# Giving each tile of the split weight ring its own offset in SBUF

## Chip, cores and metric

One core of a Trainium2 chip runs the whole kernel. The metric is the device time of one execution in microseconds.

## What is computed

One decoder layer in float32 over 256 tokens of width 2048. Three token mixers share one input projection, and their results are gated, added and projected; a SwiGLU feed-forward of width 5632 follows. Cut to what matters:

```python
h = rms_norm(x, attn_norm_g)
da_q, da_k, da_v, r_q, r_k, r_v, r_g, m_q, gates = split(h @ w_in)        # w_in: 2048 x 13312
o_da  = diff_attention(da_q, da_k, da_v, ...)      # causal, 8 heads, two softmax maps each
o_ret = retention(r_q, r_k, r_v, r_g, ...)         # 8 heads, chunks of 128
o_mem = memory_attention(m_q, mem @ w_mem_kv, ...) # 4 heads of 256
merged = sum(sigmoid(gate_b) * (o_b @ w_o_b) for b in (da, ret, mem))
x = x + merged @ w_out
hf = rms_norm(x, ffn_norm_g)
out = x + (silu(hf @ w_ffn_gate) * (hf @ w_ffn_up)) @ w_ffn_down
```

## The kernel before

Nearly all work is products of 256 tokens with float32 weight matrices. Each product is done at the rate of the rounded format fp32r and nearly to float32 accuracy: a value is split into a rounded part ("hi") and the remainder ("lo"), and hi x hi, hi x lo and lo x hi are added in PSUM (`three_passes`, the matmul of L1010).

The tokens' columns are the stationary operand. They lie transposed in `hT_hi`, `hT_lo` (normed input of a projection) and `oT_hi`, `oT_lo` (outputs of the mixers, then activations), each `[128, 16, 256]`; a block of 128 tokens by 128 columns of k is 512 bytes in each partition. The weights are the moving operand and go through a ring of four slots (`RING`). A slot holds a pair: two tiles of 128 rows (k) by 512 columns, 2,048 bytes a tile in each partition. There are three rings: `raw` as loaded, `w_hi` rounded, `w_lo` the remainder.

For each pair g, in slot s % 4:

- SyncE's queue waits until VectorE has made the remainder of pair g-4 (`lo_done`) and loads 512 KB into `raw` (L212);
- ScalarE waits for the load and until TensorE has used pair g-4 (`pair_used`), and copies `raw` to `w_hi`, which rounds it (`high`, L337; L374 for the first four);
- VectorE waits for that and writes `raw` - `w_hi` into `w_lo` (`low`, L625; L658 for the first four);
- TensorE waits for that (`lo_done`) and issues 12 matmuls: two tiles of the pair (k), two blocks of tokens (t), three passes (n). In each tile the order is hi x hi, hi x lo, lo x hi, so `w_hi`, `w_lo`, `w_hi`.

There are 584 pairs: 32 for the memory's keys and values, 16 + 96 for the projections of the mixers, 3 x 48 for gates and output projections, 32 for `w_out`, and 264 for the feed-forward (16 at its start, ten steps of 24, 8 at its end). Between pairs, at fixed places of the pair loops, stand the small matmuls and the transposes of the attention parts (L1032, L1070, L1085 and others) and, on ScalarE and VectorE, evacuations and softmax work. TensorE's output goes to two accumulators of two PSUM banks each.

The tensors `raw`, `w_hi`, `w_lo`, `hT_hi`, `hT_lo`, `oT_hi`, `oT_lo` are allocated first, in this order, at 16 KB a partition each, then `proj` (the projections, 56 KB), `kvm` and the small ones. Every tile of the rings is then a multiple of 2,048 bytes from the ring's start, and the tensors are multiples of 16,384 bytes apart.

Of the kernel before, what the change touches and what calls it, by code (L numbers as in the profile page):

```python
# [26 lines left out]
F32 = mybir.dt.float32  # L27
F32R = mybir.dt.float32r
I32 = mybir.dt.int32
ALU = mybir.AluOpType  # L30
ACT = mybir.ActivationFunctionType
AX = mybir.AxisListType

P = 128
# [3 lines left out]
NCOL = 512  # L38
# [18 lines left out]
RING = 4  # L57
# [8 lines left out]
ROUND = 12582912.0  # L66


def shape_constants():

    da = np.float32(DA_THETA) ** (-np.arange(DA_ROT // 2, dtype=np.float32) * np.float32(2.0) / np.float32(DA_ROT))
    rt = np.float32(RT_THETA) ** (-np.arange(RT_D // 2, dtype=np.float32) * np.float32(2.0) / np.float32(RT_D))
    lg = np.log(np.float32(1.0) - np.float32(2.0) ** (np.float32(-5.0) - np.arange(RT_H, dtype=np.float32)))
    return np.concatenate([da, rt, lg]).astype(np.float32)[None, :]


def program(nc, x, mem, positions, w_in, da_q_norm_g, da_k_norm_g, da_lambda_q1, da_lambda_k1,
# [6 lines left out]
    with ExitStack() as ctx:  # L84
        def sb(name, shape, dt=F32):
            return ctx.enter_context(nc.sbuf_tensor(name, shape, dt))
# [3 lines left out]


        raw = sb("raw", [P, RING, 2, NCOL])
        w_hi = sb("w_hi", [P, RING, 2, NCOL], F32R)
        w_lo = sb("w_lo", [P, RING, 2, NCOL], F32R)
        hT_hi = sb("hT_hi", [P, KD, TOK], F32R)
        hT_lo = sb("hT_lo", [P, KD, TOK], F32R)
        oT_hi = sb("oT_hi", [P, KD, TOK], F32R)
        oT_lo = sb("oT_lo", [P, KD, TOK], F32R)
        proj = sb("proj", [P, TB, GATE0])
        kvm = sb("kvm", [P, TB, D])  # L100
        sq = sb("sq", [P, TB, 2, 256])
# [55 lines left out]
        acc = [ctx.enter_context(nc.psum_tensor(f"acc{i}", [P, TB, NCOL], F32)) for i in range(2)]  # L157
        at = ctx.enter_context(nc.psum_tensor("at", [P, 4, 512], F32))
# [3 lines left out]
        hi_done, lo_done = sem("hi_done"), sem("lo_done")  # L162
# [167 lines left out]
        def _(act):  # L330
            def high(g, s):


                act.wait_ge(loaded[s % RING],
                            (g // RING + 2) * 16 if isinstance(g, int) else g * 4 + (32 - 4 * (s % RING)))
                act.wait_ge(pair_used, g + 1)
                act.activation(w_hi[:, s % RING], raw[:, s % RING], ACT.Copy).then_inc(hi_done, 1)  # L337

            def row_squares(k, t, ready, c0):

# [30 lines left out]

            for s in range(RING):
                act.wait_ge(loaded[s], 16)
                act.activation(w_hi[:, s], raw[:, s], ACT.Copy).then_inc(hi_done, 1)  # L374
                if s == 0:
                    act.wait_ge(gains_in, 16)
                    act.wait_ge(memT_in[0], 16)
                    high_input(0, range(2), oT_hi, memT)
                for n in range(1, 4):
                    if MEM_PIECES[n][0] == 2 + 2 * s:  # L380
                        act.wait_ge(memT_in[n], 16)
                high_input(0, range(2 + 2 * s, 4 + 2 * s), oT_hi, memT)


            for s in range(32):
# [8 lines left out]
                if s in (13, 15, 23, 31):  # L394
                    if s == 13:
                        act.wait_ge(row_root, 2)
                    n = (s - 6) // 8 if s == 13 else s // 8
# [27 lines left out]
            with act.Fori(0, MEM_H) as i:  # L425
                for s in range(16):
# [11 lines left out]
                    if s == 6:  # L438
                        act.wait_ge(M["negmax"], i + 1)
                        for t in range(TB):  # L440
                            e = act.activation(pm[:, t, 0:256], at[:, 2, t * 256:(t + 1) * 256], ACT.Exp,
                                               bias=nmx[:, 0, t:t + 1], scale=MEM_D ** -0.5,
                                               accum_out=den[:, 0, t:t + 1])
# [72 lines left out]
            with act.Fori(0, 4) as i:  # L516
                for s in range(12):
                    if s == 0:
                        for j in range(2):
                            e = act.activation(dec[:, j, 0:256], rel[:], ACT.Exp,  # L520
                                               scale=sc[:, ds(i * 2 + (NROT + j), 1)])
# [94 lines left out]
        def _(v):  # L616
# [5 lines left out]
            def low(g, s):  # L622

                v.wait_ge(hi_done, g + (RING + 1))
                v.tensor_tensor(w_lo[:, s % RING], raw[:, s % RING], w_hi[:, s % RING].bitcast(F32),  # L625
                                ALU.subtract).then_inc(lo_done, 1)

            def row_means(k):
# [26 lines left out]

            for s in range(RING):
                v.wait_ge(hi_done, s + 1)
                v.tensor_tensor(w_lo[:, s], raw[:, s], w_hi[:, s].bitcast(F32), ALU.subtract).then_inc(lo_done, 1)  # L658
                low_input(0, range(2 + 2 * s if s else 0, 4 + 2 * s), oT_lo, oT_hi, memT)

            for s in range(32):
# [49 lines left out]
            with v.Fori(0, MEM_H) as i:  # L711
                for s in range(16):
                    if s == 0:
# [3 lines left out]
                        for t in range(TB):  # L717
                            for k, src in enumerate((proj[:, t, ds(i * MEM_D + MQ0, MEM_D)],
                                                     kvm[:, t, ds(i * MEM_D, MEM_D)])):
                                e = v.scalar_tensor_tensor(out=qn[:, t, k, :], in0=src,  # L720
                                                           scalar=rstd[:, 2 * t + k:2 * t + k + 1],
                                                           in1=g_mem[:, k, :], op0=ALU.mult, op1=ALU.mult)
# [212 lines left out]
            for s in range(32):  # L935
# [4 lines left out]
                if s % 8 == 7:  # L940
                    n = s // 8
# [64 lines left out]
        def _(pe):  # L1006
            def three_passes(s, hi, lo, k0, p, k, t, first, last):
                tok = slice(t * P, (t + 1) * P)
                for n, (a, w) in enumerate(((hi, w_hi), (hi, w_lo), (lo, w_hi))):
                    e = pe.matmul(acc[p][:, t, :], a[:, k0 + k, tok], w[:, s % RING, k, :],  # L1010
                                  start=first and k == 0 and n == 0, stop=last and k == 1 and n == 2)
                return e

# [265 lines left out]
```

## Time and profile before

| | |
|---|---|
| median of 3 runs | 1676.9 us (1676.47 to 1677.61) |
| span of the profiled execution, first to last instruction | 1674.9 us |
| TensorE matmuls busy | 1668.0 us, 7,592 |
| VectorE busy | 950.0 us (57%) |
| ScalarE busy | 774.7 us (46%) |
| bytes read from HBM | 317.31 MB, 191 GB/s over the span |

The profiled execution's own device time isn't given apart from its span; the median of the runs lies 2.0 us above the span, which is what lies around it. Busy matmuls are pipelined and overlap, so a busy TensorE says only that it has work at all times, and the distance between the starts of two matmuls is what one costs.

### The profile page before, as it was taken

To read this page: it belongs to the slowest core of one execution; us is meant where nothing else is said; L and a number is where in the kernel's file an instruction comes from. 1 tells how busy PE (TensorE), PEld (TensorE's weight loads), DVE (VectorE), ACT (ScalarE), POOL (GpSimd) and SP (SyncE) were. 2 spreads that over 40 slices of the span, in tenths; PEclk is the share of its full clock that TensorE was granted. 3 is DMA by queue.
4 is the path that set the end of the run, shared out by engine and by line. 5 is a ranking of instruction groups with operands and counts; after the bars stand their busy time and mean duration, and the time that the engine had idled before them with its cause. 6 is when DMAs were issued, how large, how long until landed. Compare 5 with 4: busy or idle time off the path is not lost.

```text
span 1674.9 us, 21891 instructions
## 1 busy us (share of the span) xinstructions
PE 1668.0 (100%) x7592; PEld 1381.3 (82%) x7592; DVE 950.0 (57%) x1061; ACT 774.7 (46%) x936; POOL 31.9 (2%) x33
## 2 busy tenths in 40 slices
PE   9999999999999999999999999999999999999999
PEld 7888888888888888888888888888888888888887
DVE  5565554454577766655555545565554554655555
ACT  6655454444555544444444544444434444444342
POOL 0000000000111000000000000000000000000000
PEclk9999999999999999999999999999999999999999
DMA  9876555566544565666655666666666666666664
GB/s 340 265 217 187 176 169 168 177 196 192 174 152 150 180 185 175 213 199 190 188 184 184 186 189 192 191 193 188 188 192 190 190 192 188 189 192 191 192 189 151
DMA packets 167095, 319.96 MB, mean 191 GB/s; under 512 B 11152, under 2 KB 15760, under 8 KB 166288
## 3 DMA queue, kind: packets, MB, share of 16 engines
q1 hardware_dynamic: 167056, 319.45, 62.1%
q8 instruction: 24, 0.39, 0.1%
q14 instruction: 15, 0.12, 0.0%
HBM read 317.31 MB, written 2.10 MB: 191 GB/s over the span
## 4 chain that ended last, share of the span: by engine, by line
PE 91%; issue 7%; DVE 1%; DMA 0%; POOL 0%; ACT 0%; DVEq 0%; ACTq 0%; SPq 0%; POOLq 0%
PE acc L1010 87%; PE at L1032 2%; POOL rstd L315 0%; PE at L1070 0%; PE at L1085 0%; DMA raw<-in_w_mem_kv 0%; DVE w_lo L625 0%; DMA raw<-in_w_in 0%; ACT pm L486 0%; PE at L1160 0%; DVE ss L650 0%; ACT w_hi L337 0%; PE at L1172 0%; PE at L1173 0%; PE at L1171 0%
## 5 line engine op out<-in xcount | busy, mean ns | idle before, releaser
L625 DVE TENSOR_TENSOR w_lo<-raw,w_hi 128x1024 fp32r<-128x1024 f32 x580 | 706.7, 1224 | 639.5 <-ACT w_hi L337 637.6
L337 ACT ACTIVATE w_hi<-raw 128x1024 fp32r<-128x1024 f32 x580 | 614.6, 1061 | 829.4 <-PE acc L1010 812.7
L1010 PE MATMUL acc<-w_hi,hT_hi 128*128 128x512 f32 x1568 | 616.7, 393 | 0.0
L1010 PE MATMUL acc<-w_hi,hT_lo 128*128 128x512 f32 x1568 | 611.0, 390 | 0.0
L1010 PE MATMUL acc<-w_lo,hT_hi 128*128 128x512 f32 x1568 | 610.5, 389 | 0.0
L1010 PEld LDWEIGHTS acc<-w_hi,hT_hi 128*128 128x128 f32 x1568 | 294.5, 188 | 62.2 <-issue 1.3
L1010 PEld LDWEIGHTS acc<-w_hi,hT_lo 128*128 128x128 f32 x1568 | 294.4, 188 | 61.9
L1010 PEld LDWEIGHTS acc<-w_lo,hT_hi 128*128 128x128 f32 x1568 | 294.6, 188 | 59.8
L1010 PE MATMUL acc<-w_hi,oT_hi 128*128 128x512 f32 x768 | 300.9, 392 | 1.2 <-DVE oT_lo L644 1.2
L1010 PE MATMUL acc<-w_hi,oT_lo 128*128 128x512 f32 x768 | 299.1, 389 | 0.0
L1010 PE MATMUL acc<-w_lo,oT_hi 128*128 128x512 f32 x768 | 299.0, 389 | 0.0
L1010 PEld LDWEIGHTS acc<-w_hi,oT_hi 128*128 128x128 f32 x768 | 144.2, 188 | 31.4 <-issue 1.6
L1010 PEld LDWEIGHTS acc<-w_hi,oT_lo 128*128 128x128 f32 x768 | 144.2, 188 | 30.1
L1010 PEld LDWEIGHTS acc<-w_lo,oT_hi 128*128 128x128 f32 x768 | 144.3, 188 | 29.4
L927 DVE TENSOR_TENSOR proj<-acc,proj 128x1024 f32<-128x1024 f32 x47 | 57.6, 1225 | 20.6 <-PE acc L1010 20.6
L315 POOL TENSOR_TENSOR rstd<-ms,minus_half 128x4 f32<-128x4 f32 (+1 forms) x16 | 26.9, 1680 | 613.4 <-DVE ms L651 613.4
L365 ACT ACTIVATE proj<-acc,row_rstd 128x512 f32 (+1 forms) x28 | 17.7, 685 | 23.6 <-PE acc L1010 23.6
L951 DVE SCALAR_TENSOR_TENSOR proj<-acc,row_rstd,proj 128x512 f32<-128x512 f32 x22 | 15.5, 747 | 5.9 <-PE acc L1010 5.9
L1032 PEld LDWEIGHTS at<-ident,proj 128*128 128x128 f32 x120 | 14.0, 140 | 2.0
L1032 PE MATMUL at<-ident,proj 128*128 128x128 f32 x120 | 15.5, 272 | 0.0
L650 DVE TENSOR_REDUCE ss<-sq 128x4 f32<-128x512 f32 (+2 forms) x16 | 15.1, 946 | 0.0
L472 ACT ACTIVATE proj<-acc,half_rstd 128x512 f32<-128x512 f32 x24 | 15.1, 681 | 0.0
(151 smaller groups left out, 474.9 us busy)
## 6 DMA issues: line engine op xcount, KB each, us to landing
raw<-in_w_in SPq DMA_DIRECT2D x208, 512.0 KB, 3.9
raw<-in_w_ffn_gate SPq DMA_DIRECT2D x88, 512.0 KB, 3.8
raw<-in_w_ffn_up SPq DMA_DIRECT2D x88, 512.0 KB, 3.7
raw<-in_w_ffn_down SPq DMA_DIRECT2D x88, 512.0 KB, 3.8
raw<-in_w_mem_kv SPq DMA_DIRECT2D x32, 512.0 KB, 6.5
raw<-in_w_out SPq DMA_DIRECT2D x32, 512.0 KB, 3.8
raw<-in_w_o_mem SPq DMA_DIRECT2D x16, 512.0 KB, 5.3
raw<-in_w_o_da SPq DMA_DIRECT2D x16, 512.0 KB, 5.0
```

The lines of the kernel that those rows point to most:

```text
L315: nc.gpsimd.tensor_tensor(rstd[:, 0:n], ms[:, 0:n], minus_half[:, 0:n], ALU.pow).then_inc(done, 1)
L337: act.activation(w_hi[:, s % RING], raw[:, s % RING], ACT.Copy).then_inc(hi_done, 1)
L365: e = act.activation(dst[:, t], acc[p][:, t, :], ACT.Copy, scale=row_rstd[:, norm, t:t + 1])
L472: e = act.activation(sg[:, t], acc[0][:, t, :], ACT.Tanh, scale=half_rstd[:, t:t + 1])
L625: v.tensor_tensor(w_lo[:, s % RING], raw[:, s % RING], w_hi[:, s % RING].bitcast(F32), ALU.subtract).then_inc(lo_done, 1)
L650: step(v.tensor_reduce(ss[:, 0:n], src, AX.X, ALU.add), X[summed], i + 1)
L927: v.tensor_tensor(dst, acc[p][:], dst, ALU.add).then_inc(acc_free[p], 1)
L951: e = v.scalar_tensor_tensor(out=gt[:, t], in0=acc[1][:, t, :], scalar=row_rstd[:, 2, t:t + 1], in1=sg[:, t], op0=ALU.mult, op1=ALU.mult)
L1010: e = pe.matmul(acc[p][:, t, :], a[:, k0 + k, tok], w[:, s % RING, k, :], start=first and k == 0 and n == 0, stop=last and k == 1 and n == 2)
L1032: return pe.transpose(out, src, ident[:])
```

## The change

The rings `w_hi` and `w_lo` become flat tensors, 256 and 144 columns (of 4 bytes) longer, behind a small class that computes where a tile lies. Tile j = 2 x slot + k of a ring begins at j x 512 + at[j] columns. In bytes the offsets are 0, 64, 128, 192, 256, 384, 512, 768 in `w_hi` and 0, 4, 8, 16, 32, 48, 320, 448 in `w_lo`. A matmul reads one tile, still 2,048 contiguous bytes. ScalarE and VectorE still write a slot with one instruction; its operand has two blocks of 512 with the gap between them. `raw` stays as it is.

Three tensors that nobody reads or writes are put between others: 64 bytes before `oT_hi`, 32 before `oT_lo`, 416 before `proj`. The order of instructions, their number, their waits and all sizes of work are the same on every engine; only addresses differ.

```diff
+HI_AT = (0, 16, 32, 48, 64, 96, 128, 192)
+LO_AT = (0, 1, 2, 4, 8, 12, 80, 112)
+
+
+class Split:
+
+    def __init__(self, buf, at):
+        self.buf, self.at = buf, at
+
+    def tile(self, s, k):
+        j = s % RING * 2 + k
+        a = j * NCOL + self.at[j]
+        return self.buf[:, a:a + NCOL]
+
+    def slot(self, s):
+        j = s % RING * 2
+        a, step = j * NCOL + self.at[j], NCOL + self.at[j + 1] - self.at[j]
+        return self.buf[:, a:a + 2 * step].rearrange("p (k n) -> p k n", k=2)[:, :, 0:NCOL]
...
-        w_hi = sb("w_hi", [P, RING, 2, NCOL], F32R)
-        w_lo = sb("w_lo", [P, RING, 2, NCOL], F32R)
+        w_hi = Split(sb("w_hi", [P, 8 * NCOL + 256], F32R), HI_AT)
+        w_lo = Split(sb("w_lo", [P, 8 * NCOL + 144], F32R), LO_AT)
         hT_hi = sb("hT_hi", [P, KD, TOK], F32R)
         hT_lo = sb("hT_lo", [P, KD, TOK], F32R)
+        sb("oT_hi_shift", [P, 16])
         oT_hi = sb("oT_hi", [P, KD, TOK], F32R)
+        sb("oT_lo_shift", [P, 8])
         oT_lo = sb("oT_lo", [P, KD, TOK], F32R)
+        sb("proj_shift", [P, 104])
...
-                act.activation(w_hi[:, s % RING], raw[:, s % RING], ACT.Copy).then_inc(hi_done, 1)
+                act.activation(w_hi.slot(s), raw[:, s % RING], ACT.Copy).then_inc(hi_done, 1)
...
-                v.tensor_tensor(w_lo[:, s % RING], raw[:, s % RING], w_hi[:, s % RING].bitcast(F32),
+                v.tensor_tensor(w_lo.slot(s), raw[:, s % RING], w_hi.slot(s).bitcast(F32),
                                 ALU.subtract).then_inc(lo_done, 1)
...
-                    e = pe.matmul(acc[p][:, t, :], a[:, k0 + k, tok], w[:, s % RING, k, :],
+                    e = pe.matmul(acc[p][:, t, :], a[:, k0 + k, tok], w.tile(s, k),
                                   start=first and k == 0 and n == 0, stop=last and k == 1 and n == 2)
```

The first four pairs of ScalarE and VectorE (L374, L658) are changed in the same way.

## Rows read from the trace of the kernel before

**Rows 1.** The page: span, TensorE's busy time, granted clock in 40 slices.

```profile
span 1674.9 us, 21891 instructions
PE 1668.0 (100%) x7592; PEld 1381.3 (82%) x7592; DVE 950.0 (57%) x1061; ACT 774.7 (46%) x936; POOL 31.9 (2%) x33
PEclk9999999999999999999999999999999999999999
```

**Rows 2.** The page: the chain that ended last, by line.

```profile
PE acc L1010 87%; PE at L1032 2%; POOL rstd L315 0%; PE at L1070 0%; PE at L1085 0%; DMA raw<-in_w_mem_kv 0%; DVE w_lo L625 0%; DMA raw<-in_w_in 0%; ACT pm L486 0%; PE at L1160 0%; DVE ss L650 0%; ACT w_hi L337 0%; PE at L1172 0%; PE at L1173 0%; PE at L1171 0%
```

**Rows 3.** The page: costliest groups, the ring's matmuls (xcount | busy us, mean ns).

```profile
L1010 PE MATMUL acc<-w_hi,hT_hi 128*128 128x512 f32 x1568 | 616.7, 393 | 0.0
L1010 PE MATMUL acc<-w_hi,hT_lo 128*128 128x512 f32 x1568 | 611.0, 390 | 0.0
L1010 PE MATMUL acc<-w_lo,hT_hi 128*128 128x512 f32 x1568 | 610.5, 389 | 0.0
...
L1010 PE MATMUL acc<-w_hi,oT_hi 128*128 128x512 f32 x768 | 300.9, 392 | 1.2 <-DVE oT_lo L644 1.2
L1010 PE MATMUL acc<-w_hi,oT_lo 128*128 128x512 f32 x768 | 299.1, 389 | 0.0
L1010 PE MATMUL acc<-w_lo,oT_hi 128*128 128x512 f32 x768 | 299.0, 389 | 0.0
```

**Rows 4.** Chain in order of time: start us, us, what.

```profile
712.77 108.84 PE acc L1010 x480
...
1061.97 65.33 PE acc L1010 x288
```

**Rows 5.** Waits, TensorE's and its weight loads' (us in total, times, longest).

```profile
PE at L1032 <- POOL ident L299: 2.0, 1, 2.0
PE acc L1010 <- DVE oT_lo L644: 1.2, 1, 1.2
...
PEld acc L1010 <- issue: 2.9, 5, 1.6
```

**Rows 6.** Timeline of TensorE, quiet stretch: start us, us, what (the 17th follows the dots).

```profile
1159.76 0.39 PE L1010 MATMUL acc<-w_hi,hT_lo 128*128 128x512 f32 x1
1159.99 0.39 PE L1010 MATMUL acc<-w_hi,hT_hi 128*128 128x512 f32 x1
...
1163.39 0.39 PE L1010 MATMUL acc<-w_hi,oT_hi 128*128 128x512 f32 x1
```

**Rows 7.** Instructions on tile w_hi: duration ns min/median/max, first and last start.

```profile
L1010 PEld LDWEIGHTS acc<-w_hi,hT_hi x1568: 186/188/192, 95.9 to 1670.2; 128*128 128x128 f32 x196
...
L1010 PE MATMUL acc<-w_hi,hT_lo x1568: 387/389/398, 96.6 to 1670.9; 128*128 128x512 f32 x196
```

**Rows 8.** Line 1085, plain fp32 matmuls: one burst in the timeline; durations.

```profile
221.16 1.89 PE L1085 MATMUL at<-qn,pm 128*128 128x256 f32 x8
...
L1085 PE MATMUL at<-qn,pm x32: 376/379/380, 172.7 to 319.5; 128*128 128x256 f32 x32
```

**Rows 9.** Timeline of TensorE behind eight transposes (nine starts left out at the second dots).

```profile
295.79 1.03 PE L1032 MATMUL at<-ident,qn 128*128 128x128 f32 x8
...
296.89 0.39 PE L1010 MATMUL acc<-w_lo,hT_hi 128*128 128x512 f32 x1
...
299.20 0.39 PE L1010 MATMUL acc<-w_hi,hT_lo 128*128 128x512 f32 x1
```

**Rows 10.** Groups by form, ScalarE and VectorE.

```profile
L337 ACT ACTIVATE w_hi<-raw 128x1024 fp32r<-128x1024 f32 x580 | 614.6, 1061 | 829.4 <-PE acc L1010 812.7 <-DMA raw<-in_w_in 13.0 <-DMA raw<-in_w_mem_kv 3.7
...
L625 DVE TENSOR_TENSOR w_lo<-raw,w_hi 128x1024 fp32r<-128x1024 f32 x580 | 706.7, 1224 | 639.5 <-ACT w_hi L337 637.6
L927 DVE TENSOR_TENSOR proj<-acc,proj 128x1024 f32<-128x1024 f32 x47 | 57.6, 1225 | 20.6 <-PE acc L1010 20.6
```

**Rows 11.** Timeline of one round in a feed-forward step, in brackets the idle time before.

```profile
1001.29 1.06 ACT L337 ACTIVATE w_hi<-raw 128x1024 fp32r<-128x1024 f32 x1 [1.66 <-PE acc L1010]
...
1002.38 1.23 DVE L625 TENSOR_TENSOR w_lo<-raw,w_hi 128x1024 fp32r<-128x1024 f32 x1 [1.50 <-ACT w_hi L337]
```

More of the change, by code:

```diff
@@ L373, in _ @@
                 act.wait_ge(loaded[s], 16)
-                act.activation(w_hi[:, s], raw[:, s], ACT.Copy).then_inc(hi_done, 1)
+                act.activation(w_hi.slot(s), raw[:, s], ACT.Copy).then_inc(hi_done, 1)
                 if s == 0:
@@ L657, in _ @@
                 v.wait_ge(hi_done, s + 1)
-                v.tensor_tensor(w_lo[:, s], raw[:, s], w_hi[:, s].bitcast(F32), ALU.subtract).then_inc(lo_done, 1)
+                v.tensor_tensor(w_lo.slot(s), raw[:, s], w_hi.slot(s).bitcast(F32), ALU.subtract).then_inc(lo_done, 1)
                 low_input(0, range(2 + 2 * s if s else 0, 4 + 2 * s), oT_lo, oT_hi, memT)
```

## The prediction

> **What bounds the kernel now.** [...] The chain that ended last is 87% the line of the ring's matmuls [rows 2]. The grouped instructions show how many these are: three passes of 1,568 matmuls with the hT columns as weights and three of 768 with the oT columns, 7,008 in all, each streaming one 512-column tile of `w_hi` or `w_lo` [rows 3]. The busy time of one (389 to 393 ns) is no price, since neighbours overlap; the price is the distance between starts. The chain in order of time gives it: 288 matmuls of a feed-forward step take 65.33 us, so 226.8 ns each (nine of the ten steps have such a piece, of 65.30 to 65.33 us), and in an earlier stretch 480 take 108.84 us, again 226.8 ns [rows 4]. So 7,008 x 226.8 = 1589 us of 1674.9 us are matmuls that stream ring tiles. TensorE hardly waits: its matmuls wait 3.2 us on others, and the largest sum of its weight loads' waits is 2.9 us [rows 5].
>
> That makes the question simple: **does the distance of 226.8 ns depend on the address at which the tile begins?** One ns on all of them is 7.0 us. A measurement of this kernel can tell 0.2%, 3.4 us, from no change, and that is 0.48 ns per matmul.
>
> **What the trace says of addresses.** Before, every moving tile begins at a multiple of 2,048 bytes from the ring's start, and every weight block at a multiple of 512 bytes. The 16 moving tiles (slot and half), both token blocks of a weight (512 bytes apart), its k blocks (1,024 bytes apart) and three passes all share one distance: in the timeline of a quiet stretch the starts are 0.22 or 0.23 us apart from pass to pass, and 16 matmuls in a row take 3.63 us, 226.9 ns each [rows 6]; the passes have the same median duration, 389 ns [rows 7]. [...] Differences below 512 bytes occur nowhere in the trace; there the change is new.
>
> Two rows do show that 226.8 is not the smallest distance possible. Eight matmuls of 256 columns in plain fp32, each of which runs as two passes, take 1.89 us; less one duration of 379 ns, seven distances of 216 ns are left, for two steps a column and so again 512 steps (the program issues four, the trace has eight) [rows 8]. So a ring matmul spends 11 ns that those do not. And after eight transposes the ring's matmuls run at 231 ns for ten distances (296.89 to 299.20 us) before they settle [rows 9]: the distance has a state that is not set by data, operands or waits. The next such distances are 226.8 again.
>
> **The change, part by part.** *The instruction streams.* Every engine issues the same instructions in the same order with the same waits; only operand addresses differ, and the form of the operand that writes or reads a slot, now two blocks of 512 with a gap. 0 us.
>
> *ScalarE's rounding copy and VectorE's subtraction (584 each).* They write a slot as two blocks. Today they take 1,061 and 1,224 ns on a contiguous 1,024; a VectorE operation of the same size whose operand has two blocks of 512 far apart (`proj`, one row block per token half) takes 1,225 ns [rows 10]. For ScalarE the bounds are 0 and a few tens of ns. Whatever it is, it lies beside matmuls: in each round of 2.72 us ScalarE stands idle 1.66 us before its copy and VectorE 1.50 us before its subtraction [rows 11]. Each would have to become over 1.4 us longer before the rate of the ring changed; then ScalarE would be the bound. 0 us. A fp32 store that starts 4 or 8 bytes off is likewise covered unless it doubles the time (2.45 us, still inside 2.72 us).
>
> *The weight blocks.* If the tensors lie one behind another, hT_hi and hT_lo move by 1,600 bytes, oT_hi by 1,664, oT_lo by 1,696 and all behind by 2,112. A weight load takes 188 ns and never more than 192 [rows 7], 35 ns less than the distance of two matmuls, so it has room. 0 us. The DMAs into `proj` land 2,112 bytes, 33 x 64, further on; nobody on TensorE's path waits for them in the stages behind. 0 us.
>
> *The moving tiles.* Each lo tile is read by 7,008 / 3 / 8 = 292 matmuls, each hi tile by 584. The hi tiles keep multiples of 64 bytes. Of the lo tiles two (4 and 8 bytes) leave a 16-byte grid, and five (4, 8, 16, 32, 48 bytes) a 64-byte one. The rows of before have no such tile, so I bound it. Below: 0, an aligned and an unaligned tile stream alike. Above: reading at half rate, as the plain fp32 matmuls do, two steps a column; that makes 512 columns cost 2 x 216 = 432 ns, 205 ns more, on 584 matmuls 120 us. Between them lies one memory granule more per tile. With granules of 16 bytes that is 226.8 / 128 = 1.8 ns on 584 matmuls, 1.0 us; with 64 bytes 226.8 / 32 = 7.1 ns on 1,460 matmuls, 10.3 us. I take the nearest to what is seen, that addresses don't matter, and put 0.3 us for a granule that is sometimes not hidden.
>
> [...]
>
> The **sum**: 1674.9 us of span + 0 + 0 + 0.3 = 1675.2 us. The median of the runs lies 2.0 us above the profiled span (1676.9 us), so 1677.2 us.
>
> **The rivals.**
> 1. *One granule more (slower).* The matmul is held back by the fetch of its moving tile, and a tile off a 64-byte grid needs 33 fetches for 32. Place: the passes that read `w_lo` in five of eight tiles. Price: +10.3 us, 1687.2 us; with 32-byte granules (4, 8, 16 and 48 bytes, 1,168 matmuls of 3.5 ns) +4.1 us, 1681.0 us. It decides from 0.48 ns per matmul on the mean. For it: the 11 ns above the two-pass matmuls are 32 steps of about a third of a ns each, and 2,048 bytes are just 32 x 64. [...] Chance 0.11.
> 2. *The settled state is lost (slower).* Rows 9 show 231 ns while TensorE's stream is out of step. If the step depends on the distance between weight block and moving tile, it now differs from matmul to matmul and never settles: 4.3 ns x 7,008 = +30 us, 1707 us. Against it: the disturbance follows transposes and pauses and dies out, though addresses go on changing by 512 bytes and more. Chance 0.06.
> 3. *Half rate at 4 and 8 bytes (slower).* +120 us, 1797 us. Chance 0.04.
> 4. *The 11 ns are a collision of equal phases (faster).* A weight load begins in step with the matmul before it, and both walk through their rows from the same place within 512 bytes. If that costs the 11 ns, staggering removes it: 11.0 x 7,008 = -77 us, 1600 us, and half of that (1638 us) if only some offsets help. Against it: a load takes 186 to 192 ns beside any matmul [rows 7], so it shows no sign of being held up itself; and its walk is slower than the matmul's, so a shifted start would only move the place where they meet. Chance 0.13, some 0.03 of it for a gain under 5 us.
> [...]
> 5. *The change does less than it says*: a tile whose offset is 0 (the first of each ring) stands as before. That only brings the time nearer to no change.
>
> **How the numbers follow.** No measurable change: 0.65. Slower by over 0.2%: 0.11 + 0.06 + 0.04 = 0.21; faster 0.13; 0.01 for small gains in the same class goes to faster, so 0.14. The time is that of the likeliest case, 1677.2 us; its own range is 1674 to 1680 us. The range for 8 in 10 leaves out rival 3 (0.04) and the large part of rival 4 (0.10): it begins at 1673 us and ends at 1708 us, behind rival 2.
>
> **What would show each step.** Right: in the chain in order of time a feed-forward step's 288 matmuls again take 65.3 us, and in the timeline every tile of the ring has starts 0.22 or 0.23 us apart. Rival 1: the passes with `w_lo` are longer apart in the tiles off the grid and those with `w_hi` are not, 65.3 us becoming 65.7. Rival 2: distances of 224 to 237 ns all along, 66.5 us for 288. Rival 3: pairs of matmuls in slots 0 and 1 at over 400 ns. Rival 4: distances of about 216 ns, 62.2 us for 288, with ScalarE's idle time before the copy shrinking by 0.13 us per round. The ScalarE and VectorE durations of rows 10 should stay within 10 ns; were they over 2 us, my cover would be gone. The forecast is wrong if the 288 matmuls leave 65.2 to 65.5 us.

## The result, and the profile after

The change is slower: 1712.0 us (median of 4 runs, 1711.93 to 1713.32) against 1677.0 us, a ratio of 1.021 with an interval of 1.0195 to 1.0224. That it is slower is clear; on which side of 2% it lies is not. The span of the profiled execution grew from 1674.9 to 1710.2 us, by 35.3 us.

The page of the changed kernel, beside [rows 1]: span, busy time, granted clock.

```profile
span 1710.2 us, 21891 instructions
PE 1703.3 (100%) x7592; PEld 1384.3 (81%) x7592; DVE 951.1 (56%) x1061; ACT 774.6 (45%) x936; POOL 28.8 (2%) x33
PEclk9999999999999999999999999999999999999999
```

The same 21,891 instructions run, the granted clock is again at 9 tenths or more in all 40 slices, and all the added time is in TensorE's row. Its weight loads, VectorE and ScalarE are as busy as before to within 3 us.

The chain in order of time (start us, us, what), the pieces that answer to [rows 4], and one more step to show that all are alike:

```profile
725.62 111.50 PE acc L1033 x480
...
1082.71 66.90 PE acc L1033 x288
...
1150.48 66.90 PE acc L1033 x288
```

480 matmuls take 111.50 us where they took 108.84, and 288 take 66.90 where they took 65.33: **232.3 ns from start to start instead of 226.8**. The 5.5 ns times 7,008 would make 38 us. The matmuls behind transposes were at 231 ns before already [rows 9]. Added up over the whole trace, the distances between ring matmuls grew by 36.6 us and all else of TensorE's row shrank by 1.3 us, which is the 35.3 us.

TensorE still waits for almost nobody, 3.4 us in all instead of 3.2. Its waits, which answer to [rows 5]:

```profile
PE at L1055 <- POOL ident L322: 2.0, 1, 2.0
PE acc L1033 <- DVE oT_lo L667: 1.2, 1, 1.2
PE acc L1033 <- DVE w_lo L681: 0.2, 1, 0.2
```

And the two producers of the ring, by form, which answer to [rows 10]:

```profile
L360 ACT ACTIVATE w_hi<-raw 128x1024 fp32r<-128x1024 f32 x580 | 614.7, 1060 | 864.6 <-PE acc L1033 852.1 <-DMA raw<-in_w_mem_kv 7.8 <-DMA raw<-in_w_in 4.6
...
L648 DVE TENSOR_TENSOR w_lo<-raw,w_hi 128x1024 fp32r<-128x1024 f32 x580 | 707.2, 1225 | 673.8 <-ACT w_hi L360 671.6
```

1,060 and 1,225 ns against 1,061 and 1,224: the operand of two blocks costs these engines nothing, and neither do VectorE's stores to tiles that start 4 and 8 bytes off (the longest of the 580 takes 1,231 ns). Both stand idle longer before them, 864.6 and 673.8 us where it was 829.4 and 639.5: ScalarE waits for TensorE, VectorE for ScalarE. They follow TensorE, they don't hold it.

The timeline of TensorE in a quiet stretch, beside [rows 6], shows what kind of slowness it is:

```profile
1090.23 0.39 PE L1033 MATMUL acc<-w_hi,hT_hi 128*128 128x512 f32 x1
1090.45 0.40 PE L1033 MATMUL acc<-w_lo,hT_hi 128*128 128x512 f32 x1
1090.69 0.40 PE L1033 MATMUL acc<-w_hi,hT_lo 128*128 128x512 f32 x1
1090.92 0.39 PE L1033 MATMUL acc<-w_hi,hT_hi 128*128 128x512 f32 x1
1091.15 0.40 PE L1033 MATMUL acc<-w_lo,hT_hi 128*128 128x512 f32 x1
...
1093.93 0.39 PE L1033 MATMUL acc<-w_lo,hT_hi 128*128 128x512 f32 x1
```

The distances are 0.22, 0.24, 0.23, 0.23 us, and the 16 from 1090.23 to 1093.93 make 3.70 us (231 ns each; 3.63 us before). They differ from matmul to matmul, between some 225 and 240 ns, in the passes with `w_hi` as much as in those with `w_lo` (in the feed-forward steps 232.1, 232.3 and 232.6 ns in the mean behind hi x hi, hi x lo and lo x hi on hT). So it isn't a slower read of a few bad tiles. It looks like the second rival's picture, a stream that never settles, but that is only half of it. Here are three starts of this stretch and the same three places one round of the ring (48 matmuls) later:

```profile
1091.62 0.39 PE L1033 MATMUL acc<-w_hi,hT_hi 128*128 128x512 f32 x1
1091.84 0.40 PE L1033 MATMUL acc<-w_lo,hT_hi 128*128 128x512 f32 x1
1092.08 0.39 PE L1033 MATMUL acc<-w_hi,hT_lo 128*128 128x512 f32 x1
...
1102.77 0.39 PE L1033 MATMUL acc<-w_hi,hT_hi 128*128 128x512 f32 x1
1102.99 0.40 PE L1033 MATMUL acc<-w_lo,hT_hi 128*128 128x512 f32 x1
1103.23 0.39 PE L1033 MATMUL acc<-w_hi,hT_lo 128*128 128x512 f32 x1
```

In the starts to the nanosecond, a distance in the hT part of a feed-forward step and the one 48 matmuls further on differ by 0.7 ns in the mean and by 3 ns at most; 12, 24 or 36 matmuls apart they differ by about 4. The uneven distances are thus a fixed pattern with the period of the ring, set by where the operands lie.

### The profile page after: what moved, and what is told of

The parts are those of the page before. It is cut to its first block, busy times and chain, and to the rows that moved or that the text cites. A ratio compares the mean times of both kernels' runs of the same rounds, so it can differ in the third digit from the quotient of the medians.

```text
span 1710.2 us, 21891 instructions
## 1 busy us (share of the span) xinstructions
PE 1703.3 (100%) x7592; PEld 1384.3 (81%) x7592; DVE 951.1 (56%) x1061; ACT 774.6 (45%) x936; POOL 28.8 (2%) x33
## 4 chain that ended last, share of the span: by engine, by line
PE 99%; DMA 0%; SPq 0%; DVE 0%; ACT 0%; issue 0%
PE acc L1033 95%; PE at L1055 2%; DMA raw<-in_w_mem_kv 0%; PE at L1108 0%; PE at L1093 0%; PE at L1144 0%; PE at L1142 0%; PE at L1183 0%; PE at L1160 0%; PE at L1196 0%; PE at L1159 0%; PE at L1195 0%; PE at L1194 0%; PE at L1158 0%; SPq L246 0%; DVE w_lo L681 0%
## 5 line engine op out<-in xcount | busy, mean ns | idle before, releaser
L648 DVE TENSOR_TENSOR w_lo<-raw,w_hi 128x1024 fp32r<-128x1024 f32 x580 | 707.2, 1225 | 673.8 <-ACT w_hi L360 671.6
L360 ACT ACTIVATE w_hi<-raw 128x1024 fp32r<-128x1024 f32 x580 | 614.7, 1060 | 864.6 <-PE acc L1033 852.1
L1033 PE MATMUL acc<-w_hi,hT_hi 128*128 128x512 f32 x1568 | 624.1, 398 | 0.0
L1033 PE MATMUL acc<-w_hi,hT_lo 128*128 128x512 f32 x1568 | 619.5, 395 | 0.0
L1033 PE MATMUL acc<-w_lo,hT_hi 128*128 128x512 f32 x1568 | 618.5, 394 | 0.0
L1033 PE MATMUL acc<-w_hi,oT_lo 128*128 128x512 f32 x768 | 303.4, 395 | 0.0
L1033 PE MATMUL acc<-w_lo,oT_hi 128*128 128x512 f32 x768 | 303.2, 395 | 0.0
L950 DVE TENSOR_TENSOR proj<-acc,proj 128x1024 f32<-128x1024 f32 x47 | 57.6, 1225 | 23.5 <-PE acc L1033 23.5
```

The costliest lines, as they stand in the source:

```text
L360: act.activation(w_hi.slot(s), raw[:, s % RING], ACT.Copy).then_inc(hi_done, 1)
L648: v.tensor_tensor(w_lo.slot(s), raw[:, s % RING], w_hi.slot(s).bitcast(F32), ALU.subtract).then_inc(lo_done, 1)
L950: v.tensor_tensor(dst, acc[p][:], dst, ALU.add).then_inc(acc_free[p], 1)
L1033: e = pe.matmul(acc[p][:, t, :], a[:, k0 + k, tok], w.tile(s, k), start=first and k == 0 and n == 0, stop=last and k == 1 and n == 2)
```

## The experiments

Three theories stood at the start. A: the distance depends on where the weight block starts relative to the moving tile. B: it is the jump of the start from one moving tile to the next. C: tiles off a grid of 16 or 64 bytes are read slower. In all diffs below, columns are 4 bytes. "At the match" means that weight blocks and moving tiles start at the same place modulo 256 bytes, as everywhere in the kernel before.

### Weights moved alone

```diff
+        sb("hT_hi_shift", [P, 400])
         hT_hi = sb("hT_hi", [P, KD, TOK], F32R)
         hT_lo = sb("hT_lo", [P, KD, TOK], F32R)
+        sb("oT_hi_shift", [P, 16])
         oT_hi = sb("oT_hi", [P, KD, TOK], F32R)
+        sb("oT_lo_shift", [P, 8])
         oT_lo = sb("oT_lo", [P, KD, TOK], F32R)
+        sb("proj_shift", [P, 104])
```

> The kernel before with only the weight blocks (hT, oT) and what lies behind them moved by as much as in the change; the rings as before. Theory A (the distance of two matmuls depends on where the weight block starts relative to the moving tile): the hT stages run at the 233.3 ns that slot 0's first tile has in the change, where both rings' tiles are at offset 0, instead of 226.8, so over 45 us of the slowdown or more, at least 1700 us. Theory B (what costs is that consecutive moving tiles start at different offsets, so that TensorE's stream never settles): nothing changes, 226.8 ns and 1677 us. Theory C (tiles at 4, 8, 16, 32 or 48 bytes off the grid of 64 are read slower): nothing changes, 1677 us.

Measured: 1718.5 us, ratio 1.025 (1.0219 to 1.0278). A feed-forward step in the chain in order of time:

```profile
1494.92 67.19 PE acc L1014 x288
```

67.19 / 288 = 233.3 ns. No moving tile differs from the kernel before, so B and C are out as the only cause, and A stands: in the hT stages the blocks are 64 bytes out of phase and on a grid of 64 bytes. It is even slower than the change (1712.0 us). Why isn't shown: the change does contain pairs at the match, but its one tile of `w_hi` that starts at the same place as the hT blocks (64 bytes, the second of slot 0) has 233.7 ns in the mean, no less than the others. Here too the distances are a fixed pattern: in the hT stages distances of 230.8 and 235.9 ns (means of the shorter and the longer ones) take turns, and 233.3 is the mean of all.

### Tiles moved alone

```diff
+        sb("hT_hi_shift", [P, 112])
         hT_hi = sb("hT_hi", [P, KD, TOK], F32R)
         hT_lo = sb("hT_lo", [P, KD, TOK], F32R)
-        sb("oT_hi_shift", [P, 16])
         oT_hi = sb("oT_hi", [P, KD, TOK], F32R)
-        sb("oT_lo_shift", [P, 8])
         oT_lo = sb("oT_lo", [P, KD, TOK], F32R)
-        sb("proj_shift", [P, 104])
```

(against the change)

> The change with only the ring tiles staggered; hT, oT and all behind stand at multiples of 16,384 bytes from where the rings begin, as before. Theory A: the distances differ from tile to tile and the mean is over 226.8 ns, time between 1685 and 1715 us, not equal to the change's pattern. Theory B: all of the slowdown, 232.3 ns, 1712 us. Theory C: 1712 us, with the passes that read w_lo in tiles 1 to 5 longer and all others at 226.8 ns.

Measured: 1705.8 us, ratio 1.0172 (1.0143 to 1.0202). Alone the weights cost 42 us, the tiles 29 us, together 35 us: the parts don't add, each of them can spoil the match by itself. (hT and oT stand 2,048 bytes further on than before, not at multiples of 16,384 bytes; that too is a multiple of 256.)

This run also shows what theory A can't say. The first tile of slot 0, at the match in both rings, and the second of slot 1, whose `w_hi` starts 192 bytes and whose `w_lo` 16 bytes off, in the timeline (start of its six matmuls, start of what follows them):

```profile
1160.41 0.39 PE L1031 MATMUL acc<-w_hi,hT_hi 128*128 128x512 f32 x1
...
1161.80 0.40 PE L1031 MATMUL acc<-w_hi,hT_hi 128*128 128x512 f32 x1
...
1164.59 0.39 PE L1031 MATMUL acc<-w_hi,hT_hi 128*128 128x512 f32 x1
...
1165.95 0.39 PE L1031 MATMUL acc<-w_hi,hT_hi 128*128 128x512 f32 x1
```

The matched tile takes 1.39 us, 231 ns a matmul; the unmatched one takes 1.36 us, 226.7 ns, and so in every undisturbed round. The phase of a matmul's own tile and block doesn't set its own distance; what went before takes part. Theory A holds for a kernel or a stage whose operands all match, not matmul by matmul.

### Two sweeps of the phase

```diff
-        hT_hi = sb("hT_hi", [P, KD, TOK], F32R)
-        hT_lo = sb("hT_lo", [P, KD, TOK], F32R)
+        hT_hi = sb("hT_hi", [P, KD, TOK + 4], F32R)[:, :, 0:TOK]
+        sb("hT_lo_shift", [P, 64])
+        hT_lo = sb("hT_lo", [P, KD, TOK + 4], F32R)[:, :, 0:TOK]
```

> The kernel before with block k of hT_hi and hT_lo moved by k x 16 bytes (rows of the tensor 16 bytes longer), rings unmoved; oT moved by 256 bytes modulo 512. Theory A: in the hT stages the distance varies with k (eight pairs of a chunk, 0 to 240 bytes), the same pairs alike in every chunk, from 226.8 ns in the first up to some 233 ns near 64 bytes; the oT stages have one distance that differs from 226.8. Theories B and C: 226.8 ns everywhere, 1677 us.

Measured: 1696.0 us, ratio 1.0114 (1.0085 to 1.0143). The first and the last of the 96 matmuls on oT in one feed-forward step, from TensorE's timeline:

```profile
1443.94 0.39 PE L1011 MATMUL acc<-w_hi,oT_hi 128*128 128x512 f32 x1
...
1465.47 0.39 PE L1011 MATMUL acc<-w_hi,oT_lo 128*128 128x512 f32 x1
```

95 distances in 21.53 us are 226.6 ns: **a shift by 256 bytes is no shift.** In the hT stages, where the block moves on by 16 bytes from k to k, the mean distance over the feed-forward steps is 226.6 ns at k = 0, 228.1 at 16 bytes, 231.8 at 32, 232.9 at 48, between 229 and 234 up to 224 bytes, and 226.7 again at 240. Each block has only 12 matmuls in a row and, as the run with the tiles alone shows, what went before takes part, so the values between aren't those of a steady phase.

The sweep by 64 bytes has `TOK + 16` for `TOK + 4`, no `hT_lo_shift`, and 32 columns before `oT_hi`.

> As the sweep by 16 bytes, with block k of hT moved by k x 64 bytes (0 to 960) and oT by 128 bytes modulo 512. Theory A: a distance that varies with k, 233 ns where the block is 64 bytes off, and if the period is 512 bytes or less, blocks 8 to 15 repeat blocks 0 to 7; possibly offsets with less than 226.8 ns (down to 216 ns, were the whole excess of 11 ns of this kind). Theories B and C: 226.8 ns everywhere, 1677 us.

Measured: 1710.1 us, ratio 1.0198 (1.0168 to 1.0228). The same two rows, oT 128 bytes out of phase:

```profile
1456.46 0.39 PE L1011 MATMUL acc<-w_hi,oT_hi 128*128 128x512 f32 x1
...
1478.62 0.39 PE L1011 MATMUL acc<-w_hi,oT_lo 128*128 128x512 f32 x1
```

22.16 us / 95 = 233.3 ns. In the hT stages the four phases (0, 64, 128, 192 bytes) repeat with k modulo 4, which again makes the period 256 bytes: 230.0, 232.9, 233.3 and 230.4 ns. No phase ran below 226.7 ns for long, so nothing of the faster rival is left here.

### Staggered, but at the match

```diff
-HI_AT = (0, 16, 32, 48, 64, 96, 128, 192)
-LO_AT = (0, 1, 2, 4, 8, 12, 80, 112)
+HI_AT = (0, 64, 64, 128, 128, 192, 192, 256)
+LO_AT = (0, 64, 64, 128, 128, 192, 192, 256)
```

(against the change; both rings 320 columns longer, no tensors between the others)

> The change's classes and staggered tiles, with every offset a multiple of 256 bytes (0 to 1,024) and hT, oT at multiples of 256 bytes. Theory A with a period of 256 bytes (226.7 ns where weight block and moving tile start at the same place modulo 256 bytes, 233.3 ns where not): 226.7 ns everywhere, 1677 us. Theory B (what costs is that consecutive moving tiles start at different places): as the change, 232 ns, about 1710 us. A period of 512 bytes or more: over 1690 us.

Measured: 1676.6 us against 1677.0, ratio 1.0 (0.9991 to 1.001).

```profile
1459.00 65.33 PE acc L1030 x288
```

This is the change with all its new code and a stagger of its own, and the time is that of the kernel before to a tenth of a per cent. B falls in the form it had: tiles may jump by multiples of 256 bytes as they like. Jumps by other distances always come with a mismatch of phase in these runs; that a mismatch is enough without any jump was shown by the weights moved alone.

### Everything moved together, in phase

If phase were all, moving rings and weights by the same amount would cost nothing. Each of the six tensors got 64 columns more and a view that begins c columns in:

```diff
-        w_hi = sb("w_hi", [P, RING, 2, NCOL], F32R)
+        w_hi = sb("w_hi", [P, 8 * NCOL + 64], F32R)[:, c:8 * NCOL + c].rearrange("p (s k n) -> p s k n", s=RING, k=2)
...
-        hT_hi = sb("hT_hi", [P, KD, TOK], F32R)
+        hT_hi = sb("hT_hi", [P, KD * TOK + 64], F32R)[:, c:KD * TOK + c].rearrange("p (k c) -> p k c", k=KD)
```

By 4 bytes (c = 1):

> The kernel before with both rings and all four weight tensors moved by 4 bytes, so that every tile and block is off the grid of 16 bytes but they start at the same place modulo 256 bytes. Theory A: 226.7 ns, 1677 us. Theory C (a tile off a grid of 16 or 64 bytes needs one fetch more): 1.8 to 7.1 ns more on every matmul, 1689 to 1727 us; were it half rate, over 3000 us.

By 8 bytes (c = 2):

> As the kernel with all moved by 4 bytes, with 8 bytes: in phase, 8 bytes past the 16-byte grid. A grid of 16 bytes that costs whatever the distance from it: 237.8 ns, 1749 us. A grid of 8 bytes: 226.7 ns, 1677 us. Something between if the cost follows how a line is cut.

By 16 bytes (c = 4):

> Both rings and all four weight tensors moved by 16 bytes, in phase with one another, off the 64-byte grid but on the 16-byte one. If the 11.1 ns of the kernel with all moved by 4 bytes come from the 16-byte grid: 226.7 ns and 1677 us. If from a grid of 32 or 64 bytes: over 1700 us, up to 1749.

By 64 bytes (c = 16) and 128 bytes (c = 32):

> Both rings and all four weight tensors moved by 64 bytes, in phase with one another. Theory R (what counts is that tile and block start at the same place modulo 256 bytes, and on a grid of 64 bytes): 226.7 ns, 1677 us. Theory P (what counts is where each starts by itself, and the places of the kernel before, multiples of 256 bytes from one another, are the good ones): 230 to 233 ns, 1705 to 1720 us, as with 16 bytes.

> The same with 128 bytes. Theory R: 226.7 ns, 1677 us. Theory P with a period of 256 bytes: 230 to 233 ns, over 1705 us; with a period of 128 bytes (which the weights moved by 128 bytes alone speak against): 1677 us.

| all moved by | median us | ratio (interval) |
|---|---|---|
| 4 bytes | 1749.5 | 1.0432 (1.0414 to 1.0449) |
| 8 bytes | 1709.1 | 1.0197 (1.018 to 1.0214) |
| 16 bytes | 1707.4 | 1.0184 (1.0167 to 1.0201) |
| 64 bytes | 1677.3 | 1.0003 (0.9993 to 1.0012) |
| 128 bytes | 1677.8 | 1.0004 (0.9994 to 1.0013) |

One feed-forward step of the kernels moved by 4 bytes, then by 64 bytes:

```profile
1591.26 68.46 PE acc L1010 x288
```

```profile
1526.71 65.31 PE acc L1010 x288
```

237.7 and 226.8 ns. So these runs show **two conditions**: the starts must agree modulo 256 bytes (weights moved alone by 64 bytes: 233.3 ns; by 256 bytes: 226.6), and a shift of everything by 4, 8 or 16 bytes breaks the good state even when they agree (237.7, 231.6 and, over the steps, 231.7 ns), while one by 64 or 128 bytes doesn't (226.7 ns in both). Where between 16 and 64 bytes the grid lies wasn't run. Theory P, that the old places are good by themselves, falls with the two last rows. In them `raw` alone stays where it was, so a clash between TensorE's reads and those of the DMAs, ScalarE or VectorE on `raw` is out as well. Nor are the other engines' accesses the cause at 4 bytes: there the distances repeat 240, 239, 234 ns, within 1 ns, whether ScalarE and VectorE work or stand idle. Theory C was right in that a grid exists, and wrong in its form: one more fetch for a tile, as it was put there, would cost the same at 4, 8 and 16 bytes; but 4 bytes cost 72 us and 8 and 16 bytes 33 and 31, which the intervals don't tell apart.

### How near to the match

hT by +16 bytes and oT by -16, with views as above, rings unmoved; then +32 and -32.

> The kernel before with hT moved by +16 bytes and oT by 240, that is -16 modulo 256. Theory A with only the exact match cheap: 233.3 ns in both kinds of stage, 1720 us. From the sweep by 16 bytes, whose blocks 1 and 15 ran at 226.7 ns inside their pair: a window round the match, 226.7 ns in both, 1677 us.

> Rings unmoved, hT +32 bytes and oT 224 bytes (-32 modulo 256) out of phase. If the match has to be closer than 32 bytes: 233.3 ns in both kinds of stage, 1720 us. If the window reaches to 32 bytes on one side, as -16 bytes ran at 226.7 ns in the feed-forward stages and +16 at 233: 226.7 ns in the oT stages, 1706 us.

Measured: 1697.3 us (ratio 1.0121, 1.01 to 1.0141) and 1719.1 us (1.0255, 1.0234 to 1.0275). At 32 bytes both kinds of stage are at 233.3 ns. At 16 bytes neither expectation holds: the steps of one run differ. In the chain in order of time:

```profile
1409.29 65.30 PE acc L1010 x288
1475.46 66.72 PE acc L1010 x288
1543.05 66.71 PE acc L1010 x288
```

The first of these three runs at 226.7 ns, the next two at 231.6, with the same instructions and addresses, and so on in threes through the loop. In the fast steps hT and oT matmuls are both at 226.7 ns once settled; in the slow ones those on hT (+16 bytes) are at 233.3 and those on oT (-16 bytes) at 228.4. Both states exist at this phase.

### Which operand, and does the next matmul pay too

One weight tensor 128 bytes out of phase (`hT_lo` in the hT stages, `oT_hi` in the oT stages), by 32 columns before each of `hT_lo` and `oT_lo`:

> The kernel before with hT_lo alone moved by 128 bytes in the hT stages, and oT_hi alone in the oT stages. Theory A, form 1 (the load that runs beside a matmul is that of the next matmul's weights, and meets its moving tile): a third of the distances in the hT stages is 6.7 ns longer, mean 228.9 ns; in the oT stages two thirds, 231.1 ns; about +20 us in all, 1697 us. Form 2 (once a load is out of step the stream loses its settled state and all distances vary): both stages near 231 to 233 ns, over 1705 us.

The ring `w_lo` alone 128 bytes out of phase, by 32 columns before `w_lo` and 32 before `hT_hi`:

> The kernel before with the ring w_lo alone moved by 128 bytes, weights and w_hi at the match. So one matmul of three (hi x w_lo) is out of phase. Form F (a distance is 6.7 ns longer when its own moving tile is out of phase with its own or with the next weights): 1 of 3 distances, mean 228.9 ns, about 1693 us. Form G (a matmul out of phase also costs the next one, which has to find its step again): 2 of 3, mean 231.1 ns, about 1708 us.

Measured: 1709.8 us (ratio 1.0196, 1.0175 to 1.0216) and 1712.2 us (1.0208, 1.0178 to 1.0237). In the first the hT stages have 226.7, 232.5 and 234.2 ns after hi x hi, hi x lo and lo x hi, and the oT stages are over 232 ns in all three. Their means are 231.1 and 233.4 ns, where form 1 had 228.9 and 231.1: form 2 is nearer, and the extra time falls on two of three distances, then on all. In the second a third of the matmuls is out of phase and nearly all distances are longer, 232.3 ns in the mean. It beats even form G's 231: **one operand out of phase takes from two thirds of the price to all of it** (`hT_lo` 4.4, `w_lo` 5.5 and `oT_hi` 6.7 ns, where a whole mismatch costs 6.6). Its steps alternate strictly, 66.56 and 67.20 us.

### Which operand minds 4 bytes

`w_lo` alone by 4 bytes; then hT by 4 and oT by 8 bytes.

> The kernel before with the ring w_lo alone moved by 4 bytes. The kernel with all moved by 4 bytes had 11.1 ns more on every matmul. If the moving tile off the 16-byte grid is what costs, one matmul of three has 11 ns more, mean 230.4 ns, about 1703 us; if the weight block is, nothing, 1677 us.

> The kernel before with hT moved by 4 and oT by 8 bytes, rings unmoved. If the weight block off the 16-byte grid is what costs the 11 ns of the kernel with all moved by 4: 237.8 ns in the hT stages and, should 8 bytes cost as 4 do, in the oT stages, 1749 us. If the moving tile is: 226.7 ns, 1677 us.

Measured: 1717.5 us (ratio 1.0239, 1.021 to 1.0269) and 1709.1 us (1.0189, 1.016 to 1.0219). Each operand, moved alone, makes the stream slower: the hT stages (4 bytes) have 232.2 ns in the mean, the oT stages (8 bytes) 230.7. With `w_lo` alone moved all three distances are longer (231, 237 and 232 ns, mean 233.3), more than the third that was expected. Moved alone, an operand is also 4 or 8 bytes out of phase with the other, so these two runs don't say how much is the grid's and how much the phase's.

### The change without its two worst tiles

```diff
-LO_AT = (0, 1, 2, 4, 8, 12, 80, 112)
+LO_AT = (0, 0, 0, 4, 8, 12, 80, 112)
```

> The change with the two w_lo tiles that begin 4 and 8 bytes past a 16-byte grid put at offset 0 instead. If being out of phase modulo 256 bytes is the whole cost: 1712 us as the change. If the two tiles off the grid have a share of their own, as the kernel with everything moved by 4 bytes has 11.1 ns per matmul while in phase: up to 584 x 11.1 ns = 6.5 us less, 1705 us.

Measured: 1710.0 us, ratio 1.0199 (1.0182 to 1.0216), where the change has 1.021 (1.0195 to 1.0224). The two intervals overlap. In the chain a feed-forward step takes 66.80 us instead of 66.90, which would be 2.4 us over all ring matmuls: the share of the tiles at 4 and 8 bytes is some 2 us or nothing, and not the 6.5 us.

### A load that walks as fast as the matmul

A guess at the mechanism, which no run shows: a weight load reads its 512 bytes while the matmul beside it reads about 1,024 (an estimate: 2,048 bytes spread evenly over the 389 ns that one lasts in the trace are 990 bytes in the 188 ns of a load), and where they meet modulo 256 bytes the stream loses a fixed time. With hi and lo interleaved, the load walks 1,024 bytes too and by this guess there is nothing to meet.

```diff
+        sb("hT_shift", [P, 32])
-        hT_hi = sb("hT_hi", [P, KD, TOK], F32R)
-        hT_lo = sb("hT_lo", [P, KD, TOK], F32R)
+        hT = sb("hT", [P, KD, TOK, 2], F32R)
+        hT_hi, hT_lo = hT[:, :, :, 0], hT[:, :, :, 1]
+        sb("oT_shift", [P, 32])
-        oT_hi = sb("oT_hi", [P, KD, TOK], F32R)
-        oT_lo = sb("oT_lo", [P, KD, TOK], F32R)
+        oT = sb("oT", [P, KD, TOK, 2], F32R)
+        oT_hi, oT_lo = oT[:, :, :, 0], oT[:, :, :, 1]
```

> hi and lo columns of the weights interleaved element by element in one tensor (a weight block is 128 columns 8 bytes apart, so a load walks 1,024 bytes instead of 512 in the same time, as fast as the matmul's tile does), hT 128 bytes out of phase with the rings, oT at the match. If the excess comes from the places where the load and the matmul meet modulo 256 bytes (they drift apart by 512 bytes in a load, so they meet two or three times, 6.7 ns each): with no drift they never meet where the phases differ, 216 ns in the hT stages, and are together all the time in the oT stages. The lo columns start 4 bytes off the grid, which may cost up to 11 ns. So 1600 to 1750 us by this theory. If only the start matters: hT 233 ns or more, oT 227 ns or more, 1700 us or more. If a strided load is slower, over 1750 us.

Measured: 1711.2 us, ratio 1.0202 (1.0172 to 1.0231); 233.4 ns in the oT stages and 231 in the hT stages, not 216. A load on hT takes 196 ns there, not 188:

```profile
L1012 PEld LDWEIGHTS acc<-w_hi,hT 128*128 128x128 f32 x3136 | 613.7, 196 | 112.5 <-issue 1.3
```

The guess gave no gain, and it isn't supported. Since the lo columns start 4 bytes off the grid, and all operands 4 bytes off in phase cost 11 ns a matmul, it isn't refuted for a layout that stays on the grid; that wasn't tried.

## Why the prediction was wrong

**Right.** The instruction streams are unchanged. The copies of ScalarE and VectorE cost 0 (1,060 and 1,225 ns) behind their cover of 1.7 and 1.5 us. Weight loads stay at 188 ns, no wait of TensorE in the trace is one on a DMA, and the granted clock is 9 tenths or more in every slice, as before. The bound was named rightly, and so was its lever: one ns on all ring matmuls is 7.0 us. All of the added time came through it.

**The step that failed** is the term "The moving tiles", put at 0.3 us, for which I took "the nearest to what is seen, that addresses don't matter". It rests on the rows by which all tiles, blocks and passes share one distance. The 0.3 us itself was my guess: no row and no run shows a granule of the memory, of 16, 32 or 64 bytes, that a tile could need once more. The runs gave 5.5 ns on a ring matmul in the mean in its place, some 37 us. The rows were right: in the starts to the nanosecond of the feed-forward steps before, each of the 16 moving tiles with each of the two token blocks has a mean distance between 226.0 and 227.1 ns. The step from them, that addresses don't matter, was not. Every address difference that the trace of before contains is a multiple of 512 bytes; the period turned out to be 256 (a shift by 256 bytes: 226.6 ns; by 128: 233.3). Differences above 512 bytes that are no multiple of 256 do matter: the 1,600 bytes by which hT moved are 64 modulo 256, and moved so alone it ran at 233.3 ns. Rows that all lie on one phase say nothing of phase, in either direction. The bounds that I set on this term, 0 to 120 us, were bounds on the read of an unaligned tile; the cost of a tile out of phase with a weight block had no bound there and stood among the rivals alone.

The term "The weight blocks", put at 0 us, failed with it. I priced only whether a load still ends in time (it does, 188 ns of 227) and not what its place does to the matmul beside it. Moved alone they cost 42 us.

**Rival 2, the settled state lost**, given 6 in 100, comes nearest. Its condition came true: "If the step depends on the distance between weight block and moving tile, it now differs from matmul to matmul". Its signs fit, distances of some 225 to 240 ns and 66.9 us for 288 where it said 224 to 237 and 66.5. The rest, "and never settles", is wrong: the stream settles into a pattern that repeats with the ring, and with a constant mismatch into a few distances that take turns. Its price, 4.3 ns and 1707 us against 5.5 ns and 1712.0, came from [rows 9], where the stream was disturbed by transposes at matching addresses. That the two sizes lie so near was luck as far as these runs show. What I held against it, that the disturbance dies out "though addresses go on changing by 512 bytes and more", was again evidence from one phase only. It should have had the chance that the question deserved, with an upper end at 233 ns or a bit more; the range ended 4 us below the result.

**Rival 1**, one fetch more per tile off a grid, is not what the change pays: it would fall on the passes with `w_lo` alone, and those with `w_hi` are lengthened as much; the two tiles off the 16-byte grid are worth some 2 us, within the intervals. **Rival 3**, half rate, is out: with everything 4 bytes off a matmul costs 237.7 ns. **Rival 5**, that the tiles at offset 0 stand as before, overlooked that the weight blocks move too: the first tile of slot 0 has 233.2 ns in the change. **Rival 4**: equal phase is the good state (226.7 ns) and not the bad one (233.3 ns with 64 or 128 bytes between), the sign was the other way round. The 11 ns between 226.7 and the 216 ns of the plain fp32 passes remain in every layout that was run. That a pass of 256 columns in plain fp32 is as much work as 512 columns here, two steps a column, was my reading; [rows 8] show only the 216 ns, and eight passes for four matmuls.

**What stays open.** The mechanism below the two conditions is not shown. It can't be a price on each mismatched matmul by itself, since a mismatched tile ran at 226.7 ns and a matched one at 231 in the kernel with the tiles moved alone. Two levels come again and again, 226.7 and 233.3 ns, but the upper one is a mean over distances that take turns (230.8 and 235.9 ns, or 229.2 and 237.5), settled stretches at 230.0 and 231.1 ns exist too, and the one attempt to use the 6.7 ns between them failed (231 ns where 216 was hoped for). Nor is it settled how the change's 35 us divide between phase and grid: five of its eight `w_lo` tiles and `oT_lo` are off the 64-byte grid too, and breaking either condition alone is enough to lose the good state (233.3 ns with the weights alone out of phase, 231.6 with all moved by 8 bytes).

## What to carry to other kernels

Where TensorE streams fp32r tiles back to back with a weight load beside each, let weight blocks and moving tiles start at the same place modulo 256 bytes, all of them on a grid of 64 bytes: here that is worth 2 to 4% (1676.6 to 1677.8 us with both kept, 1718.5 with the weights alone moved, 1707.4 to 1749.5 with all off the grid), and one tensor out of step is enough to lose most of the 2.5% that the phase is worth (1712.2 us with `w_lo` alone). It was shown for matmuls of 128x128 by 512 columns alone. A small pad before a hot tensor is therefore a change of its own; pad by multiples of 256 bytes (1676.6 us here, as before the change), and look at the distance of matmul starts (the chain's pieces divided by their counts) rather than at busy shares, which show 100% in both cases. And when a trace holds only one value of what a change varies, it bounds nothing: take the range from rows in which the engine was seen in another state.

## What was not expected of the hardware

- In the kernel with all moved by 16 bytes the nine steps of the feed-forward loop alternate strictly between two times, though each issues the same instructions on the same addresses:

```profile
1418.56 66.25 PE acc L1010 x288
1485.69 67.20 PE acc L1010 x288
1553.76 66.25 PE acc L1010 x288
```

  230.0 and 233.3 ns: the state of the stream lasts there from one interruption to the next. It changes only behind the eight transposes that stand in each step: before those at 1417.5 us the last 36 matmuls are at 233.3 ns, and behind them the stream goes to 230.0 and stays there through hT and oT until the next ones. With `w_lo` alone 128 bytes out of phase it is 66.56 and 67.20 us, and with the weights at +16 and -16 bytes one step in three is at 65.30 and two at 66.7.
- All operands 4 bytes off, in phase, cost 11 ns per matmul (1749.5 us), more than any mismatch of phase that was run (6.7 ns); 8 bytes off cost 5 ns (1709.1 us).
- The distance never fell below 226.7 ns for long in any of the layouts run, and 233.3 ns is a mean that comes again and again: the weights 64, 128 or 32 bytes out of phase all give it, though by different distances in turn (64 bytes: 230.8 and 235.9 ns; 128 bytes: 229.2 and 237.5).
